# A hybrid decoder step on one core: the fill in two segments with the norm off the projection's chain, expert slots taken one by one, and the sample tile's front dealt over two tiles

## The reference

```
xn   = rms_norm(x) * attn_norm
proj = xn @ w_in                       # q, k (rotated), v, and the 1792 columns of the time mixing
o_da = differential attention(q, k, v) # the sample rows also over 512 cached, paged keys
o_rw = RWKV-7 time mixing(p_rw)        # a state of 64 x 64 for each of 8 heads
h    = x + concat(o_da, o_rw) @ w_out
hn   = rms_norm(h)
s    = product keys of hn @ peer_wq    # 8 heads, top 16 of 128 x 128 experts for each row
out  = h + sum over 128 experts of gate * gelu(u_e . hn) * v_e
y    = rms_norm(out)
```

## Time and profile before

| | us |
|---|---|
| median of three runs | 4287.4 |
| the profiled execution | 4256.6 |
| its span, first to last instruction | 4254.8 |
| TensorE busy in the span | 2876.2 |
| VectorE | 2600.3 |
| ScalarE | 1141.1 |
| POOL | 1327.4 |
| first expert gather issued | 848.5 |

### The profile page before, as it was taken

The page is one execution under the profiler, slowest core; times in us unless marked ns, Lnnn a source line. Parts: engine busy times, 40 slices in busy tenths (PEclk is TensorE's granted clock), DMA queues, the critical chain, the costliest instruction groups (busy, mean ns, idle before and its releaser), DMA issues.

```text
span 4254.8 us, 53587 instructions
## 1 busy us (share of the span) xinstructions
PE 2876.2 (68%) x20366; PEld 1444.2 (34%) x20366; DVE 2600.3 (61%) x5836; ACT 1141.1 (27%) x3061; POOL 1327.4 (31%) x1163
## 2 busy tenths in 40 slices
PE   4688879966667566657767676667667466655554
PEld 2544454533224223423333242333324144211111
DVE  1332165288749866883987588578838534457754
ACT  0211121133323333242333324233422122222221
POOL 0000000044424433442443243334424343245543
PEclk9889989977778678878877787877877665776555
DMA  7355714599999999999999999999999667999998
GB/s 259 129 174 190 264 36 167 197 401 384 418 380 408 401 412 367 413 416 379 404 413 414 378 404 406 403 379 413 403 364 387 207 233 270 355 364 419 419 410 347
DMA packets 319382, 1445.20 MB, mean 340 GB/s; under 512 B 28228, under 2 KB 64196, under 8 KB 179478
## 3 DMA queue, kind: packets, MB, share of 16 engines
...
q1 hardware_dynamic: 157334, 284.08, 18.7%
...
...
## 4 chain that ended last, share of the span: by engine, by line
DMA 34%; PE 30%; DVE 23%; issue 5%; ACT 4%; POOL 3%; SPq 0%; DVEq 0%; ACTq 0%; POOLq 0%
DMA pe_buf<-in_experts,pe_idx 20%; DMA op_wkr<-scratch_wk_rows 10%; DVE pe_buf L2187 10%; PE ip_B L961 9%; PE pe_B L1292 4%; PE pe_psO L1342 4%; PE pe_B L1275 3%; POOL pe_buf L914 2%; PE pe_psH L1324 1%; PE pe_B L1246 1%; PE pe_B L997 1%; DMA tm_ps<-in_x 1%; ACT pe_Z L1644 1%; POOL at_vp L874 1%; DMA op_w<-in_w_out 1%
## 5 line engine op out<-in xcount | busy, mean ns | idle before, releaser
L914 POOL DMA_INDIRECT pe_buf<-in_experts,pe_idx x1088 | 1260.4, 1158 | 2750.4 <-PE pe_psO L1342 1717.0
L2187 DVE CUSTOM_DVE_ANT_0 pe_buf<-pe_buf,pe_hnR 128x1024 f32<-128x1024 f32 x1088 | 1315.1, 1223 | 886.3 <-DMA pe_buf<-in_experts,pe_idx 723.0
L1342 PE MATMUL pe_psO<-pe_buf,pe_Z 128*32 128x256 f32 x8704 | 791.6, 496 | 758.3 <-ACT pe_Z L1644 738.1
L1342 PEld LDWEIGHTS pe_psO<-pe_buf,pe_Z 128*32 128x32 f32 x8704 | 270.6, 131 | 1286.2 <-ACT pe_Z L1644 1014.6
L1636 ACT ACTIVATE pe_gelu<-pe_dot 128x2 f32<-128x2 f32 x544 | 110.2, 203 | 1678.1 <-DVE pe_dot L2187 1677.7
L961 PE MATMUL ip_B<-ip_w,ip_xT 128*128 128x512 f32 (+1 forms) x1008 | 421.7, 571 | 5.8 <-DMA ip_w<-in_w_in 4.0
L1324 PE MATMUL pe_psH<-pe_hn,pe_pick 128*128 128x512 f32 x544 | 404.0, 834 | 12.5 <-ACT pe_hnR L1606 11.0
L1292 PE MATMUL pe_B<-op_wkr,pe_mix 128*128 128x512 f32 (+1 forms) x576 | 294.9, 663 | 152.6 <-DMA op_wkr<-scratch_wk_rows 152.6
L1644 ACT ACTIVATE pe_Z<-pe_gl,pe_gelu 128x8 f32<-128x8 f32 x1088 | 267.7, 293 | 26.5 <-ACT pe_gelu L1636 1.8
L961 PEld LDWEIGHTS ip_B<-ip_w,ip_xT 128*128 128x128 f32 x1008 | 190.6, 193 | 210.8 <-issue 201.1
L1292 PEld LDWEIGHTS pe_B<-op_wkr,pe_mix 128*128 128x128 f32 (+1 forms) x576 | 115.6, 208 | 318.3 <-issue 317.8
...
## 6 DMA issues: line engine op xcount, KB each, us to landing
...
pe_buf<-in_experts,pe_idx POOLq DMA_INDIRECT x1088, 12.7
...
```

The lines of the kernel that those rows point to most:

```text
L914: pool.indirect_dma_start(buf[b][:], None, T["experts"], bass.IndirectOffsetOnAxis(ap=idx[:, t % 2, h * NJ + j:h * NJ + j + 1], axis=0)).t ...
L1342: last = nc.tensor.matmul(psO[32 * x:32 * x + 32, j // 4, :], Z[:, n % NZ, 24 - 8 * turn:56 - 8 * turn], buf[n % NBUF][:, D + x * QUART:D ...
L2187: nc.vector.tensor_tensor_reduce(buf[b][:, 0:D], buf[b][:, 0:D], hnR[:, n // PH % 2, :], 1.0, 0.0, ALU.mult, ALU.add, dot[:, n % (NBUF):n ...
```

## The change

Five things, in one diff.

- `FILL` has two segments after the first pass instead of three. The first merges one stream of the projection of tiles 1 and 2, `wk`, and the projection of tiles 3 and 4 with one of `tm`, `at` and `op` of tile 0, which begins after a gap of 12 empty steps. The costs of the stages are told apart.
- The norm leaves the chain in front of the transposes: TensorE transposes x as loaded, and the row's factor (`ip_r`) goes into the rotation table (`ip_rope`, scaled by VectorE) for rotated units and into ScalarE's copy for the others. A tile's part of `project` has three steps instead of five. Most constants are waited for at the end of the first pass instead of at the start (`first_in`, `constants`).
- ScalarE takes the gelu of one slot at a time (`gate`), and TensorE adds one slot at each slot, one behind.
- The sample tile's front is dealt over the 128 slots of tile 6 and 76 of tile 7, its attention at a cost of 3.3 a step.
- The choice for the sample tile is dealt over the slots 80 to 120 of tile 7, for the others over 2 to 120.

```
 FILL = (((("ip", (0,)),),),
-        ((("wk", None), ("ip", (1, 2))), (("tm", 0), ("at", 0))),
-        ((("ip", (3, 4)),), (("op", 0),)),
+        ((("ip", (1, 2)), ("wk", None), ("ip", (3, 4))), (("gap", 12), ("tm", 0), ("at", 0), ("op", 0))),
         ((("ip", (5, 6, 7, 8)),), (("tm", 1), ("at", 1), ("op", 1)), (("topk", 0),)))
-DURING = tuple((("tm", t), ("at", t), ("op", t)) for t in range(2, NT))
-COST = {"ip": 2.4, "wk": 1.8, "tm": 1.8, "at": 1.8, "op": 1.8, "topk": 1.8}
+WK_PASS = 2
+DURING = tuple((("tm", t + 2), ("at", t + 2), ("op", t + 2)) for t in range(LAST - 1))
+COST = {"gap": 3.0, "ip": 3.3, "wk": 1.1, "tm": 1.9, "at": 1.3, "op": 2.2, "topk": 1.8}
+COST_LAST_AT = 3.3
+LAST_OP_BY = 76
...
-TOPK_FROM, TOPK_TO = 2, 118
+TOPK_FROM, TOPK_FROM_LAST, TOPK_TO = 2, 80, 120
+ACT_LAG, SUM_LAG = 0, 1
...
     plan = []
-    for t in range(LAST):
-        costs = [COST[item[0]] for item in (DURING[t] if t < len(DURING) else ()) for _ in range(steps_of(item))]
+    for t, items in enumerate(DURING):
+        costs = costs_of(items)
         total, spent, i = sum(costs), 0.0, 0
-        for k in range(PER):
+        length = PER if t < len(DURING) - 1 else PER + LAST_OP_BY
+        for k in range(length):
...
@@ SP: in_projection @@
                     if t:
                         sp.wait_ge(ip["turned"], 2 * t)
+                        sp.wait_ge(ip["summed"], t)
+                        sp.wait_ge(ip["scaled"], t)
...
-                        sp.dma_start(dst[:], T[name]).then_inc(const_in, 16)
+                        sp.dma_start(dst[:], T[name]).then_inc(first_in, 16)
...
@@ TensorE @@
-            pe.wait_ge(const_in, 16 * CONSTS_IN)
+            pe.wait_ge(first_in, 16 * FIRST_IN)
...
-                    pe.wait_ge(ip["scaled"], t + 1)
+                    pe.wait_ge(ip["x_in"], 16 * (t + 1))
...
-                if n >= 2 and n % 2 == 0:
-                    v_sum(n - 2)
-                    v_sum(n - 1)
+                if n >= SUM_LAG:
+                    v_sum(n - SUM_LAG)
...
@@ ScalarE @@
-                            nc.scalar.activation(ip_o[:, g_ % 2, 0, 0:cols_of(n)], ipB[:, g_ % 3, 0:cols_of(n)], ACT.Copy
-                                                 ).then_inc(ip["copied"], 1)
+                            act.wait_ge(ip["scaled"], t + 1)
+                            nc.scalar.activation(ip_o[:, g_ % 2, 0, 0:cols_of(n)], ipB[:, g_ % 3, 0:cols_of(n)], ACT.Copy,
+                                                 scale=ip_r[:, 2, t:t + 1]).then_inc(ip["copied"], 1)
...
+            def gate(n):
+                col, h = n % NBUF, slots[n][2]
+                act.wait_ge(f["dotted"], n + 1)
+                nc.scalar.activation(gelu[:, col:col + 1], dot[:, col:col + 1], ACT.Gelu_apprx_tanh).then_inc(f["gelu_done"], 1)
+                if h == 0:
+                    act.wait_ge(f["gl_ready"], n // PH + 1)
+                act.wait_ge(f["gelu_done"], n + 1)
+                if n >= NZ:
+                    act.wait_ge(f["v_used"], n - NZ + 1)
+                nc.scalar.activation(Z[:, n % NZ, 24:32], gl[:, n // PH % 2, h, :], ACT.Copy,
+                                     scale=gelu[:, col:col + 1]).then_inc(f["Z_ready"], 1)
...
@@ VectorE @@
-            dve.wait_ge(const_in, 16 * CONSTS_IN)
+            dve.wait_ge(first_in, 16 * FIRST_IN)
...
-                    dve.wait_ge(ip["squared"], t + 1)
-                    chain(nc.vector.reciprocal(st[:, 2:3], st[:, 1:2]))
-                    nc.vector.tensor_scalar(ip_x[:], ip_x[:], st[:, 2:3], None, ALU.mult).then_inc(ip["scaled"], 1)
...
+                    dve.wait_ge(ip["squared"], t + 1)
+                    dve.wait_ge(ip["rope_in"], 16 * (t + 1))
+                    chain(nc.vector.reciprocal(ip_r[:, 2, t:t + 1], ip_r[:, 1, t:t + 1]))
+                    nc.vector.tensor_scalar(ip_rope[:, i].rearrange("p a d -> p (a d)"), ip_rope[:, i].rearrange("p a d -> p (a d)"),
+                                            ip_r[:, 2, t:t + 1], None, ALU.mult).then_inc(ip["scaled"], 1)
...
                     if base == 0 and u == NG:
+                        constants()
                         dve.wait_ge(ip["shift_in"], 16)
```

120 lines of the change are left out of this document (59 added, 61 removed).

## The result

| | before | changed |
|---|---|---|
| median of 20 runs each, us | 4289.2 | 4307.3 |
| ratio | 1 | 1.0037 (95%: 1.002 to 1.0055) |
| profiled execution, us | 4256.6 | 4298.1 |
| its span | 4254.8 | 4296.2 |
| first expert gather issued | 848.5 | 826.4 |

A forecast was written before the change was run, and what follows sets the result against it. It took DMA bytes to bound ordinary tiles, with holes at the sample front, and TensorE to bound the fill. Fill -46, ordinary tiles -12, sample front +3 gave -55 us: median 4232, forecast range 4195 to 4265, 8-in-10 range 4160 to 4290.

The forecast's parts named there:

- ordinary tiles: Slots of six tiles: 2 us a tile from TensorE's shorter wait for key weights, -12 us; 10 lost to 30 won.
- The sample front: Sample tile's front dealt over two tiles: longer sequences +14, outside terms -7 and -10, squeezed choice +6; +3 us in sum.
- neutral: Sample attention: a sequence of 44.9 us, 31.6 and 5.2 slots at 2.56, would be neither gain nor loss.
- the terms outside the sequences: Sample front: end of time mixing -7 us, output projection -10, squeezed choice of tile 8's experts +6.
- The first rival: Sample front: the chain of steps sets the 31.6 us, so slots fill the DMA holes; -150 in total, median 4136, chance 0.20.
- The fill: Stretch before the first expert gather: TensorE idle falls from 170 to 126 us, some 2 from the clock; 46 us gained.
- The wait for the time mixing: Fill: TensorE waits 27 us instead of 36 for the time mixing's first input, a load left on one DMA engine.
- the keys: Fill: TensorE's wait of 19 us for the load of the keys remains.
- the +6: Tile 7: choice of tile 8's experts squeezed into 40 slots, 116 us of VectorE work in 102 us of gathers; +6 us.
- the sign that was to tell the reading of the ordinary tiles wrong: Ordinary tiles: if their 382 us change by more than 5, reading them as bound by bytes is wrong.
- The slower rival: Sample front: the lead runs out at every sequence, 56 us each; fill gives only 20; +60 in total, median 4348, chance 0.12.
- Nothing is left: Whole kernel: fill gives 20 us and the front takes 15 of it; -5 to -15, 4277 us, chance 0.18.

The follow-up runs named there:

- c2: The changed kernel unaltered, measured again as a control on one chip with e15 and e16: 4309 us, 1.0049 of the kernel before.
- e15: The changed kernel with ScalarE's gelu and TensorE's sums in pairs of slots again, on the same chip as c2: 4223 us, 0.9845 of before.
- e16: The changed kernel with ScalarE's gate one slot behind instead of none, TensorE's sum still one behind, on the same chip as c2: 4250 us, 0.9901 of before.
- e3: The changed kernel with ScalarE's gelu and TensorE's sums in pairs of slots again, on another chip than e15: 4200 us, 0.9866 of before.
- e4: The changed kernel with the sample attention's page gathers five steps later in POOL's program, from the third sequence on: 4195 us, 0.9841 of before.
- e1: The changed kernel with everything in the slots as before, in pairs, leaving only the fill's two segments and the norm off the chain: 4236 us, 0.9943 of before.
- c1: The changed kernel unaltered, measured again as a control on a chip of the faster kind: 4301 us, 1.0106 of before.

## Why the prediction was wrong

**The failed step: ordinary tiles, -12 us (bounds -30 to +10).** It measured +48 in the two traces, some +20 by the estimate that allows for the chip, and either is above the bound of +10; with tile 6 the single slots cost 87 us on one chip (c2 and e15), of which 54 lie in tiles 0 to 5 of the traces. The step counted ScalarE's work, "0.1 us a slot on an engine that is a third busy", and took the DMA share of 1.00 as a reason that nothing else could change the time. That share fell to between 0.95 and 0.98 in tiles 3 to 5. It had held only because buffers came free in time; what the change moved was how close behind each slot ScalarE and TensorE wait for it. One slot of distance for ScalarE gave 60 of the 87 us back (e16). The mechanism stood in the bound as "ScalarE's chain now in front of every slot" at 10 us, and was given no price from the trace. The exponentials, where the waiting is plain to see, do not give that price: they are not later after the change than before (79 us and 91 in all). Which waits of the front grew, against before, stays open; what is shown is that pairs, or ScalarE one slot behind, take the loss away. The exchange of choice and front was not priced either, and no run has it alone with single slots.

**The sample front, +3 forecast.** Between the traces +16 (902 us for tiles 6 and 7 before, 918 now). The mechanism is as forecast, and so is its mean: values to values 49.2, 52.2, 57.0 and 37.6 us, 49.0 in the mean for 49.2, the last 41.6 for 42; neutral was 44.9. That every sequence would take 49.2 was not so, and that the mean comes so close is in part luck. From the first late gather of values to the last, 3503.66 to 3741.36, the front loses 12 us against the 159 us before and 26 more slots at 2.56; +14 was forecast. What was mis-sized are the terms outside the sequences, -11 together, which came to about +4. The term was also worked out with single slots in place, and hid that the deal is worth 26 us with pairs, where the four distances have a mean of 43.5 us (e3): with single slots it was TensorE's short distance that kept them long. The first rival (the chain sets the period and the holes fill) is refuted by e4 in its reason, not in its size: once the release no longer held POOL, the slots did fit.

**The fill, -46 forecast, -22 in the trace and -24 by e1.** TensorE's idle time fell from 170 to 147 us (826.4 less 679.5 busy), not to 126, and its busy time (678.3 before) did not fall by the 2 us taken for the clock. The timeline of TensorE in the changed kernel's fill, against the earlier trace rows:

```profile
12.35 16.10 PE L976 MATMUL ip_B<-ip_w,ip_xT 128*128 128x512 f32 x32 [3.86 <-DMA ip_w<-in_w_in]
37.38 15.54 PE L976 MATMUL ip_B<-ip_w,ip_xT 128*128 128x512 f32 x32 [8.92 <-DMA ip_w<-in_w_in]
...
89.19 1.97 PE L956 MATMUL ip_B<-pe_ident,ip_x 128*128 128x128 f32 x8 [15.15 <-DMA ip_x<-in_x]
...
166.30 0.69 PE L1032 MATMUL pe_B<-pe_ident,tm_lo 128*128 128x128 f32 x2 [31.42 <-ACT tm_lo L1439]
```

The first matmul is where it was forecast (13), but the third block lands at 37.4 and not 33, and the seventh is waited for as well, so the first pass ends at 74.0 against 84.9: 11 us for 17. The wait for the time mixing is 31.4 us for 27, the boundary ahead of it idles 21 for 19, and the keys make two waits, 11.8 and 9.1 us, for 19. That is 14 of the 21 us that are missing. The other 7 or so are short waits between 166 and 518 us, where the front now runs beside the projection as one stream; they were not followed up.

**What else the forecast said would show.** The choice's slots have a DMA share of 0.90 from 4017 on, under the 0.95 named; the 10 us that this costs are near the +6. The first expert gather came at 826.4 and not at 803, TensorE's wait at 31.4 us and not within 25 to 30. And the sign that was to tell the reading of the ordinary tiles wrong, more than 5 us on the 382, is what came: 393.

**The slower rival** had its mechanism in the wrong place (the sequences, above 53 us) and its size 40 us too high. *Nothing is left* had both its terms nearly as they came, the fill at -20 and the front at +15 (-22 and +16 between the traces), and missed the same step, the ordinary tiles.

By measured parts the change is then: fill -24, deal, new costs and the exchange of choice and front -33 (0.9866 less 0.9943, one chip), single slots +87 (one chip). That is +30, between the +16 to +21 and the +45 that the two kinds of chips show. The first two parts are from the faster kind of chip and the third from the slower, so this sum can't close better; on the faster kind the single slots cost about 100 us (c1 and e3, two chips).
